# GpSimd takes the turning back of the state tiles and half of the angles in the state-space stage of a one-core transformer kernel

## The reference: what is computed

```python
lam_bar = jnp.exp(lam * dt)                       # 32 groups x 64 states, complex
b_bar = ((lam_bar - 1.0) / lam)[..., None] * b_mat
bu = jnp.einsum('gpc,bsgc->bsgp', b_bar, ug)      # input of each state, 256 tokens
_, states = lax.associative_scan(_linear_recurrence, (a, bu), axis=1)   # s[t] = lam_bar * s[t-1] + bu[t]
y = jnp.einsum('gcp,bsgp->bsgc', c_mat, states).real
y = y + d_skip * uf
y = jax.nn.gelu(y)
y = y * jax.nn.sigmoid(y @ w_glu)
...
q = apply_rope(q, positions)                      # first half x cos - second half x sin, and so on
k = apply_rope(k, positions)
```

## Time and profile before

| | |
|---|---|
| three runs, median (lowest to highest) | 2374.36 us (2374.03 to 2378.84) |
| the profiled execution: span from first to last instruction | 2374.4 us |
| PE busy over the span | 2192.9 us, 92% |
| DVE busy | 958.4 us, 40% |
| ACT busy | 605.2 us, 25% |
| POOL busy | 19.0 us, 1% |
| mean granted TensorE clock | 0.973 |

### The profile page before, as it was taken

The page is one execution under the profiler, slowest core; times in us unless marked ns, Lnnn a source line. Parts: engine busy times, 40 slices in busy tenths (PEclk is TensorE's granted clock), DMA queues, the critical chain, the costliest instruction groups (busy, mean ns, idle before and its releaser), DMA issues.

```text
span 2374.4 us, 26405 instructions
## 1 busy us (share of the span) xinstructions
PE 2192.9 (92%) x10794; PEld 1277.1 (54%) x10794; DVE 958.4 (40%) x1689; ACT 605.2 (25%) x991; POOL 19.0 (1%) x38
## 2 busy tenths in 40 slices
PE   5989988998899999989865999989999999999998
PEld 3447742333333333333323888547887886555887
DVE  6971231221222222122213655344555553363555
ACT  3021120011000101100103443244445442164433
POOL 0000000000000000000000000000000000100000
PEclk8999989999999999999987999999999999999999
DMA  7672469999999999999995443315443543312541
GB/s 304 262 283 80 166 259 420 427 423 428 427 422 428 428 427 417 428 427 417 429 427 220 191 182 141 142 66 200 185 187 160 206 166 146 142 54 107 212 160 80
DMA packets 42925, 633.64 MB, mean 267 GB/s; under 512 B 5040, under 2 KB 5040, under 8 KB 6224
## 3 DMA queue, kind: packets, MB, share of 16 engines
q1 hardware_dynamic: 42800, 631.90, 64.9%
HBM read 630.84 MB, written 1.05 MB: 266 GB/s over the span
## 4 chain that ended last, share of the span: by engine, by line
PE 71%; DMA 18%; DVE 4%; ACT 2%; issue 2%; SPq 0%; ACTq 0%; DVEq 0%
DMA piece<-in_moe 18%; PE bank L1838 11%; PE bank L1754 10%; PE bank L1756 10%; PE bank L1755 10%; PE bank L1873 5%; PE bank L642 5%; PE bank L1285 4%; PE bank L1248 2%; PE bank L1819 2%; PE bank L1897 2%; PE bank L938 1%; PE bank L1252 1%; PE bank L1080 1%; PE bank L2168 1%
## 5 line engine op out<-in xcount | busy, mean ns | idle before, releaser
L1838 PE MATMUL bank<-piece,xeT 128*64 128x512 f32 (+1 forms) x2304 | 449.9, 625 | 61.7 <-DMA piece<-in_moe 58.7
L1760 DVE TENSOR_TENSOR ffn_lo<-slot,ffn_hi 128x2048 fp32r<-128x2048 f32 x132 | 302.1, 2292 | 170.6 <-ACT ffn_hi L2293 165.2
L1838 PEld LDWEIGHTS bank<-piece,xeT 128*64 128x64 f32 (+1 forms) x2304 | 135.4, 132 | 343.8 <-issue 321.3
L1754 PE MATMUL bank<-ffn_hi,hT_hi 128*128 128x512 f32 x704 | 280.2, 398 | 8.5 <-DVE hT_lo L566 6.0
L2293 ACT ACTIVATE ffn_hi<-slot 128x2048 fp32r<-128x2048 f32 x132 | 251.8, 1913 | 130.2 <-PE bank L1756 115.2
L1756 PE MATMUL bank<-ffn_hi,hT_lo 128*128 128x512 f32 x704 | 275.0, 391 | 0.0
L1755 PE MATMUL bank<-ffn_lo,hT_hi 128*128 128x512 f32 x704 | 274.4, 390 | 0.0
L1945 DVE TENSOR_TENSOR hT<-hT,bank 128x512 f32<-128x512 f32 x144 | 92.2, 682 | 268.1 <-PE bank L1897 261.8
L1992 DVE TENSOR_SCALAR work<-bank 128x256 f32<-128x256 f32 x60 | 25.5, 425 | 353.9 <-PE bank L1845 353.9
L1754 PEld LDWEIGHTS bank<-ffn_hi,hT_hi 128*128 128x128 f32 x704 | 132.6, 188 | 38.1 <-issue 8.5
L1756 PEld LDWEIGHTS bank<-ffn_hi,hT_lo 128*128 128x128 f32 x704 | 132.4, 188 | 28.5
(11 more groups left out here) (620 smaller groups left out, 2354.9 us busy)
## 6 DMA issues: line engine op xcount, KB each, us to landing
piece<-in_moe SPq DMA_DIRECT2D x192, 2048.0 KB, 24.4
slot<-in_ffn SPq DMA_DIRECT2D x44, 3072.0 KB, 10.3
slot<-in_ada SPq DMA_DIRECT2D x16, 1024.0 KB, 5.3
slot<-in_merge SPq DMA_DIRECT2D x4, 3072.0 KB, 12.2
slot<-in_nsa_in SPq DMA_DIRECT2D x5, 2048.0 KB, 7.3
slot<-in_ada SPq DMA_DIRECT2D x2, 3072.0 KB, 17.9
slot<-in_w_in SPq DMA_DIRECT2D x6, 1024.0 KB, 7.3
slot<-in_hy_in SPq DMA_DIRECT2D x3, 2048.0 KB, 7.7
```

Source lines behind the costliest of these rows:

```text
L1754: pe.matmul(out, left[0], right[0], start=start, stop=False)
L1760: return dve.tensor_tensor(lo, x, hi.bitcast(F32), ALU.subtract)
L1838: pe.matmul(bank[n * c:n * (c + 1), :], x[:, kt, :], w[i][:, at:at + 512], start=kt == 0, stop=False)
```

## The change

- POOL makes the arguments of quarters 2 and 3, from the moment when the rates are ready, by `ssm_angles(..., pool=True)`, which replaces each two-step instruction with two inputs by a one-input and a two-input instruction. DVE makes only quarters 0 and 1. All quarters now use `table` itself as scratch.
- POOL turns the state tiles back (`ssm_pool`), two products for a tile. DVE's scans write to one of two buffers `ssm_c` (in `rows`), and from tile 2 on a scan waits until POOL has turned tile j-2 back (`rotated`).
- DVE waits at each quarter's first tile for that quarter's sines alone (before: tile 0 waited for three quarters' sines).
- The rotation of q and k (`rotated_rows`) moves from the stage's end to behind tile 11 and behind tile 13 on DVE.

```diff
     for jj in range(SSM_Q):
+        steps.mark(eng.tensor_scalar(b[:, jj, :], time, state(14, jj), ROUND, ALU.mult, ALU.add))
+    steps.mark(eng.tensor_scalar(b, b, ROUND, None, ALU.subtract))
+    if pool:
+        for jj in range(SSM_Q):
+            steps.mark(eng.tensor_scalar(a[:, jj, :], time, state(6, jj), None, ALU.mult))
+        steps.mark(eng.tensor_tensor(a, a, b, ALU.subtract))
+        for jj in range(SSM_Q):
+            steps.mark(eng.tensor_scalar(b[:, jj, :], time, state(7, jj), None, ALU.mult))
+        steps.mark(eng.tensor_tensor(a, a, b, ALU.add))
...
+    steps.mark(eng.tensor_scalar(a, a, 0.5, -0.5, ALU.min, ALU.max))
+    if pool:
+        steps.mark(eng.tensor_scalar(b, a, 0.25, None, ALU.is_gt))
+        eng.tensor_tensor(b, b, a, ALU.subtract).then_inc(done, 1)
...
 def angles_of(k, q):
-    if q == 1:
-        scratch = k["rows"][:, 0:2 * D]
-    elif q == 3:
-        scratch = k["ring"][2][:, 4096:6144]
...
+    return k["table"][:, q, 1, :, :], k["table"][:, q, 0, :, :]
...
         if jj == 0:
-            dve.wait_ge(s["trig_done"], 6 if q == 0 else 8)
+            dve.wait_ge(s["trig_done"], 2 * q + 2)
...
+        if j >= 2:
+            dve.wait_ge(s["rotated"], 2 * (j - 1))
         for c in range(2):
-            vs.mark(dve.tensor_tensor_scan(B[:, c, :], decay, A[:, c, :], 0.0, ALU.mult, ALU.add))
-        vs.wait()
-        if j >= SSM_ROWS:
-            dve.wait_ge(s["ssm_y_ready"], (j - SSM_ROWS) // SSM_Q + 1)
-        R = ssm_rows(k, j)
-        vs.mark(dve.tensor_tensor(R[:, 0, :, :], B[:, :, :], cosb, ALU.mult))
-        dve.tensor_tensor(R[:, 1, :, :], B[:, :, :], sinb, ALU.mult).then_inc(s["rotated"], 1)
...
+            dve.tensor_tensor_scan(k["ssm_c"][:, j % 2, c, :], decay, A[:, c, :], 0.0, ALU.mult, ALU.add).then_inc(s["scanned"], 1)
+        dve.wait_ge(s["scanned"], 2 * j + 2)
...
+def ssm_pool(k, pool, tiles):
+    s = k["sig"]
+    for j in tiles:
+        q, jj = divmod(j, SSM_Q)
+        if jj == 0:
+            pool.wait_ge(s["trig_done"], 2 * q + 2)
+        pool.wait_ge(s["scanned"], 2 * j + 2)
+        if j >= SSM_ROWS:
+            pool.wait_ge(s["ssm_y_ready"], (j - SSM_ROWS) // SSM_Q + 1)
+        R = ssm_rows(k, j)
+        for trig, of in enumerate(ssm_tables(k, q)):
+            pool.tensor_tensor(R[:, trig, :, :], k["ssm_c"][:, j % 2, :, :], of(jj), ALU.mult).then_inc(s["rotated"], 1)
...
-            ssm_angles(f, dve, 2)
...
-            ssm_vector(f, dve, range(0, 3))
-            ssm_angles(f, dve, 3)
-            ssm_vector(f, dve, range(3, 6))
+            ssm_vector(f, dve, range(0, 6))
...
-            ssm_vector(f, dve, range(11, 16))
+            ssm_vector(f, dve, range(11, 12))
+            rotated_rows(0)
+            ssm_vector(f, dve, range(12, 14))
+            rotated_rows(1)
+            ssm_vector(f, dve, range(14, 16))
...
+            pool.wait_ge(s["small_loaded"], 48)
+            pool.wait_ge(s["ssm_prep_dve"], 1)
+            for q in range(2, 4):
+                ssm_angles(f, pool, k["pos"], q, s["trig_pool"], True)
+            ssm_pool(f, pool, range(SSM_TILES))
             end_phase(k, pool, 2)
```

More of the change, by code:

```diff
@@ L793, in ssm_prep_scalar, with ssm_angles @@
     act.activation(k["ssm_small"][:, 5 * n:6 * n], k["ssm_small"][:, 13 * n:14 * n], ACT.Sin).then_inc(s["ssm_prep_act"], 1)
-def ssm_angles(k, dve, q):
-    s, vs, n = k["sig"], k["vs"], SSM_TILES
+def ssm_angles(k, eng, steps, q, done, pool=False):
+    n = SSM_TILES
     time = con(k, "time")
     a, b = angles_of(k, q)
-    if q == 2:
-        dve.wait_ge(s["trig_done"], 2)
     def state(i, jj):
@@ L809, in ssm_angles @@
     for jj in range(SSM_Q):
-        vs.mark(dve.tensor_scalar(b[:, jj, :], time, state(14, jj), ROUND, ALU.mult, ALU.add))
-    vs.wait()
[L812 to L818, removed]
@@ new lines, in ssm_angles @@
+    steps.wait()
+    steps.mark(eng.tensor_scalar(b, b, ROUND, None, ALU.subtract))
+    if pool:
+        for jj in range(SSM_Q):
+            steps.mark(eng.tensor_scalar(a[:, jj, :], time, state(6, jj), None, ALU.mult))
+        steps.wait()
+        steps.mark(eng.tensor_tensor(a, a, b, ALU.subtract))
+        steps.wait()
+        for jj in range(SSM_Q):
+            steps.mark(eng.tensor_scalar(b[:, jj, :], time, state(7, jj), None, ALU.mult))
+        steps.wait()
+        steps.mark(eng.tensor_tensor(a, a, b, ALU.add))
+    else:
+        steps.wait()
+        for jj in range(SSM_Q):
+            steps.mark(eng.scalar_tensor_tensor(out=a[:, jj, :], in0=time, scalar=state(6, jj), in1=b[:, jj, :], op0=ALU.mult, op1=ALU.subtract))
+        steps.wait()
+        for jj in range(SSM_Q):
+            steps.mark(eng.scalar_tensor_tensor(out=a[:, jj, :], in0=time, scalar=state(7, jj), in1=a[:, jj, :], op0=ALU.mult, op1=ALU.add))
@@ L837, in ssm_trig_scalar @@
+    steps.wait()
+    steps.mark(eng.tensor_scalar(a, a, 0.5, -0.5, ALU.min, ALU.max))
+    steps.wait()
+    if pool:
+        steps.mark(eng.tensor_scalar(b, a, 0.25, None, ALU.is_gt))
+        steps.wait()
+        eng.tensor_tensor(b, b, a, ALU.subtract).then_inc(done, 1)
+    else:
+        eng.scalar_tensor_tensor(out=b, in0=a, scalar=0.25, in1=a, op0=ALU.is_gt, op1=ALU.subtract).then_inc(done, 1)
+def angles_of(k, q):
+    return k["table"][:, q, 1, :, :], k["table"][:, q, 0, :, :]
 def ssm_trig_scalar(k, act, q):
@@ L838, in ssm_trig_scalar @@
     s = k["sig"]
-    act.wait_ge(s["trig_arg"], q + 1)
+    act.wait_ge(*((s["trig_arg"], q + 1) if q < 2 else (s["trig_pool"], q - 1)))
     a, b = angles_of(k, q)
@@ L851, in ssm_rows, with ssm_tables @@
     return k["ring"][i // 2][:, at:at + 1024].rearrange("p (a b c) -> p a b c", a=2, b=2)
+def ssm_tables(k, q):
+    return tuple(lambda jj, trig=trig: spread(k["table"][:, q, trig, jj, :], 2) for trig in range(2))
 def ssm_vector(k, dve, tiles):
@@ L860, in ssm_vector @@
         if jj == 0:
-            dve.wait_ge(s["trig_done"], 6 if q == 0 else 8)
-        cosb = spread(k["table"][:, q, 0, jj, :], 2)
-        sinb = spread(k["table"][:, q, 1, jj, :], 2)
+            dve.wait_ge(s["trig_done"], 2 * q + 2)
+        cosb, sinb = (of(jj) for of in ssm_tables(k, q))
         bu = k["ps"][4 + j % 2][:, :].rearrange("p (a b) -> p a b", a=2)
@@ L3067, in program @@
         k["ada_r"] = work[:, 1024:2560].rearrange("p (a b) -> p a b", a=3)
+        k["ssm_c"] = k["rows"][:, 4 * D:5 * D].rearrange("p (i a b) -> p i a b", i=2, a=2)
         mix = ExitStack()
@@ L3341, in _ @@
             angles_vector(f, dve)
-            ssm_angles(f, dve, 0)
-            ssm_angles(f, dve, 1)
+            ssm_angles(f, dve, k["vs"], 0, s["trig_arg"])
+            ssm_angles(f, dve, k["vs"], 1, s["trig_arg"])
             ada_vector(f, dve, 0)
```

28 lines of the change are left out of this document (8 added, 20 removed).

## The result

The changed kernel takes 2392.62 us (median of 5 runs, 2384.43 to 2393.95) against 2374.15 us (5 runs, 2373.75 to 2378.84): ratio 1.0053, 95% interval [1.0035, 1.0071]. (The ratio and its interval are those on record for the runs; the two medians divided give 1.0078.) The forecast was 2386.2 us with 2366 to 2400 as range, slower with chance 0.71. One thing has to be set right first: where a run has both numbers, its time is 1.7 to 1.9 us longer than its span (here 2393.95 against 2392.1), so a sum that starts at the span of before, 2374.4 us, gives a span and not a time.

What follows compares the result with a forecast made beforehand. It took DVE to pace the start and PE the tile loop, and summed 2374.4 - 6.9 (quarter 3's arguments) - 0.7 (first steps) + 17.0 (POOL beside DVE's start) + 2.4 (rotation) = 2386.2 us, range 2366 to 2400.

Steps and rivals of the forecast that it cites:

- What bounds: First 170 us: DVE paces the start, PE the tile loop, and a shift of the stage's end shifts the whole kernel.
- Quarter 3's arguments leave the loop, -6.9: Tile loop: PE's 4.63 us wait for DVE and the slow clock behind it (2.3 us) go, gain 6.9 us.
- First steps, -0.7: First loop steps, paced by DVE's 4.9 us: two or three gain 0.3 us each as products leave DVE, 0.7 us.
- POOL's arguments beside DVE's start, +17.0: Start: POOL and DVE block each other on the shared port, so PE's projection starts 17 us later.
- a copy is nearest and I take its slope: Price of POOL's one-input arithmetic instructions, which no row showed: a copy's 0.82 ns a column.
- the walk: Both engines' lists priced by turns: DVE reaches conditioning at 52.4 us, POOL's arguments end at 42; PE waits up to 4.8 late.
- Dearer POOL: Rival, chance 0.18: POOL's one-input instructions cost 1.3 ns a column or more, start loses 22 to 31 us, time 2391 to 2400.
- The rotation, +2.4: Loop: moved rotation is paid from DVE's slack; PE waits up to 4.8 us ahead of last outputs, middle taken, 2.4.
- the first term: Tile loop: the 6.9 us gain from quarter 3's arguments leaving, which counted 2.3 us of slow clock behind the wait.
- The sum: Whole kernel: 2374.4 - 6.9 - 0.7 + 17.0 + 2.4 = 2386.2 us, 0.5% slower.
- a microsecond of its end is a microsecond of the kernel: Stages behind the state-space stage: they hold nothing of the change, so any shift of its end passes whole to the total.

Runs made afterwards that it cites:

- e8: Kernel before, nothing on POOL, DVE making quarter 3's arguments in two pieces behind tiles 6 and 8: 2375.56 us, ratio 0.9999.
- e9: Kernel before, nothing on POOL, DVE making quarter 3's arguments in three pieces (ahead of the uT copy, behind tiles 6 and 10): 2377.07 us, ratio 0.9998.
- e4: Changed kernel with the rotation of q and k back at its old place: 2384.67 us, ratio 1.0029.
- e7: Changed kernel with the products back on DVE and the rotation at its old place, so POOL makes only the arguments: 2387.40 us, ratio 1.0045.
- e1: Changed kernel with POOL's arguments held back until the first third of the conditioning is done: 2398.16 us (one run).
- e2: Changed kernel with an idle second operation added to POOL's one-operation one-input instructions: 2395.40 us (one run).
- e11: Kernel before with only the products moved to POOL, arguments on DVE and rotation at their old places: 2377.38 us, ratio 1.0009.

## Why the prediction was right or wrong

*What bounds.* Right in its chain (line 357 at the start, PE in the loop, everything behind the stage shifts with it). Incomplete: "both are nearly full, but PE is fuller" missed that DVE's list through the whole loop ends only 1 us ahead of PE's last outputs, so that it is probably the second bound; e8 and e9 fit that.

*Quarter 3's arguments leave the loop, -6.9.* Right: -6.8 in the changed kernel, -6.9 from the first inputs to the stage's end in e4 and e7. *First steps, -0.7*: not there. From the first inputs to tile 5's, PE took 24.40 us before, 19.77 without its wait, and 19.70 after.

*POOL's arguments beside DVE's start, +17.0.* The mechanism is shown (e1 takes it away, e7 has it alone). The size was 12.4, and the step that failed is "a copy is nearest and I take its slope" for all one-input instructions: ten of a quarter's fifteen are forms that cost 0.9 us at 256 and 2.8 at 1024 columns, and these hold DVE up little. The changed kernel's own rows show it: beside a 2.37 us product DVE came 2.1 us behind its old pace, beside the four slow multiplies that follow (4.24 us) 0.8 us. So POOL's arguments ended at 64 us, not 42; part of them fell behind line 357, where only the mixing matrices met them, beside PE's projection. e2 shows the direction: with the multiplies fast, line 357 comes later. That it comes at 52.89 us, beside the walk's 52.4, is partly luck, since POOL ended at 58.9 us there and the walk had it end at 42. "Dearer POOL" had the price right and the direction wrong: a dearer instruction was assumed to hold DVE for as long as it lasts.

*The rotation, +2.4.* The walk gave 4.8 with blocking; I took the middle against its own result, and left out the lower clock that was seen behind the wait in the loop, though the first term counted it. It measured 4.75 + 1.8 = 6.6 (6.7 between after and e4, from the first inputs on).

*The sum.* For the stage I had +11.8 us, and 12.1 came out. That is luck: 4.6 us too many at the start and 4.2 too few at the end cancel, with 0.8 us of gain in the loop that didn't come. The total was 6.4 us above my 2386.2. Of this 1.8 us are the span that was taken for a time. Nearly all the rest arose behind the stage, where "a microsecond of its end is a microsecond of the kernel" was taken as exact: "behind" ranges over 9 us between kernels that are the same there, and the sum was made against an execution with nearly the shortest. Some 3.5 to 4 us are the piece with two values; the others scatter in the code ahead of it and behind it. Why an execution falls on one or the other side is not settled, nor whether the change itself has a share: no run changed only this. The changed kernel took 2391.87 to 2394.25 us in ten of its eleven runs, and once 2384.43.

## What to carry to other kernels

Before giving DVE's work to POOL, look at what DVE does while POOL works: at a place where DVE's list is the path, POOL's arguments cost 12.5 us, and 18 us when their multiplies were made faster (e2); in a loop whose pace is PE's POOL's products were free (e11). Moving work about within a full list moved the wait and removed little of it (e8, e9). Take a bound at its own value: halving it "in the middle" cost 2.4 of the 4.2 us that the rotation's term was short. And look at more than one execution of the kernel before, where the total is to be told to a few microseconds.

## What was not expected of the hardware

- On POOL a one-operation multiply over 128x1024 took 2.77 us, multiply and add 1.04, minimum and maximum 1.04, but subtract and add 3.65 and the comparison, with or without an addition, 2.8 to 3.6 us (these last two only beside DVE's work, in e2 and in the changed kernel).
- Beside the slow form DVE's 128x256 product took 0.57 us, beside the fast one 1.04, beside POOL's product 1.72, on average; alone 0.43. The slow form doesn't leave DVE wholly alone: a cast of 0.16 us took 1.00 us beside POOL's subtraction at 16 us.
- POOL's product of a tensor with itself took 1.89 us, of two different ones mostly 2.34 to 2.40, both 128x1024. (The second also writes over one of its inputs, so the number of tensors read isn't the only difference.)
- POOL's idle time between two marks in untouched code had one of two values, 505.1 or 509 us: the same scores ran at a granted clock of 1.00 or of 0.50, with PE's starts alike within 0.02 us up to them in the traces of before and after.
